# A new order of the sparse-attention stage: turns, conversions and top-k rounds at other places in four queues

## What is computed

```python
h = rms_norm(x, norm_g[l])
proj = h @ w_in[l]
(..., q_b, k_b, v_b, z_b, qi, ki, wi, q_m, z_m, gate) = jnp.split(proj, cuts, axis=-1)
qb = rotary(rms_norm(q_b.reshape(B, S, 8, 128), dsa_q_norm_g[l]), positions)
kb = rotary(rms_norm(k_b.reshape(B, S, 8, 128), dsa_k_norm_g[l]), positions)
y_b = dsa_attention(qb, kb, vb, qib, kib, wib).reshape(B, S, 1024) * jax.nn.silu(z_b)
merged = (g[:, :, 0] * (y_a @ w_branch[l, 0]) + g[:, :, 1] * (y_b @ w_branch[l, 1])
          + g[:, :, 2] * (y_m @ w_branch[l, 2]))
```

## Time and profile before

| | us |
|---|---|
| median of 3 runs | 975.56 |
| lowest, highest | 972.61, 975.66 |
| the profiled execution | 975.56 |
| its span, first to last instruction | 973.5 |
| TensorE busy | 957.0 (98%) |
| VectorE busy | 718.6 (74%) |
| ScalarE busy | 534.5 (55%) |
| GpSimd busy | 351.6 (36%) |
| mean granted TensorE clock | 0.998 |

### The profile page before, as it was taken

The page is one execution under the profiler, slowest core; times in us unless marked ns, Lnnn a source line. Parts: engine busy times, 40 slices in busy tenths (PEclk is TensorE's granted clock), DMA queues, the critical chain, the costliest instruction groups (busy, mean ns, idle before and its releaser), DMA issues.

```text
span 973.5 us, 13407 instructions
## 1 busy us (share of the span) xinstructions
PE 957.0 (98%) x4897; PEld 840.1 (86%) x4897; DVE 718.6 (74%) x1079; ACT 534.5 (55%) x810; POOL 351.6 (36%) x247
## 2 busy tenths in 40 slices
PE   8999999999899999999998999999999999999998
PEld 7888888888778988988987878898998989988887
DVE  6878987686996696696696466796776867735486
ACT  6877645454447547546563321676675857741351
POOL 0200835457055164164130053271623626106600
PEclk9999999999999999999999999999999999999999
DMA  8624222143532432432363234707024150638312
GB/s 282 238 87 130 88 87 87 43 146 115 155 95 65 149 111 66 143 114 70 119 217 130 94 128 157 238 12 215 1 86 142 32 152 1 234 92 310 142 44 86
DMA packets 105156, 119.27 MB, mean 123 GB/s; under 512 B 4772, under 2 KB 80136, under 8 KB 104332
## 3 DMA queue, kind: packets, MB, share of 16 engines
q1 hardware_dynamic: 105084, 118.53, 37.3%
q10 hardware_dynamic: 16, 0.00, 0.0%
HBM read 106.45 MB, written 12.07 MB: 122 GB/s over the span
## 4 chain that ended last, share of the span: by engine, by line
PE 87%; DVE 8%; issue 2%; ACT 1%; DMA 1%; POOL 0%; SPq 0%; DVEq 0%; ACTq 0%
PE proj L780 39%; PE proj L1289 9%; PE proj L1140 9%; PE att L1310 7%; PE proj L1310 5%; PE att L1360 3%; PE proj L950 2%; PE att L1122 2%; PE att L1104 1%; DVE score L2396 1%; PE att L1069 1%; DVE small L2394 1%; PE proj L1246 1%; PE att L1112 1%; PE att L1047 1%
## 5 line engine op out<-in xcount | busy, mean ns | idle before, releaser
L780 PE MATMUL proj<-hT_hi,w_hi 128*128 128x512 f32 x328 | 129.0, 393 | 0.0
L780 PE MATMUL proj<-hT_hi,w_lo 128*128 128x512 f32 x328 | 128.0, 390 | 0.0
L780 PE MATMUL proj<-hT_lo,w_hi 128*128 128x512 f32 x328 | 127.8, 390 | 0.0
L2131 DVE TENSOR_TENSOR w_lo<-w_raw,w_hi 128x2048 fp32r<-128x2048 f32 x28 | 68.6, 2449 | 49.9 <-ACT w_hi L1410 45.8
L1410 ACT ACTIVATE w_hi<-w_raw 128x2048 fp32r<-128x2048 f32 x28 | 53.6, 1914 | 67.7 <-PE proj L780 66.4
L780 PE MATMUL proj<-y_hi,w_hi 128*128 128x512 f32 x192 | 76.2, 397 | 4.9 <-DVE merged L2665 3.3
L780 PE MATMUL proj<-y_lo,w_hi 128*128 128x512 f32 x192 | 75.4, 393 | 0.0
L780 PE MATMUL proj<-y_hi,w_lo 128*128 128x512 f32 x192 | 75.3, 392 | 0.0
L780 PEld LDWEIGHTS proj<-hT_hi,w_lo 128*128 128x128 f32 x328 | 61.5, 188 | 13.0
L780 PEld LDWEIGHTS proj<-hT_lo,w_hi 128*128 128x128 f32 x328 | 61.6, 188 | 12.3
L780 PEld LDWEIGHTS proj<-hT_hi,w_hi 128*128 128x128 f32 x328 | 61.6, 188 | 12.2
(11 more groups left out here) (522 smaller groups left out, 2935.5 us busy)
## 6 DMA issues: line engine op xcount, KB each, us to landing
w_raw<-w_in_in SPq DMA_DIRECT2D x36, 512.0 KB, 4.3
w_raw<-w_in_in SPq DMA_DIRECT2D x56, 256.0 KB, 3.5
w_raw<-w_branch_in SPq DMA_DIRECT2D x10, 1024.0 KB, 5.2
merged<-w_in_in SPq DMA_DIRECT2D x38, 256.0 KB, 3.5
merged<-w_in_in SPq DMA_DIRECT2D x14, 512.0 KB, 5.8
...
```

Of the source, the lines that this page charges most:

```text
L780: ins = mm(ps, lhs[a](k, k0), rhs[b](k, k0), start=(first and k == 0 and j == 0), stop=(last and k == KH - 1 and j == 2))
L2131: V.tensor_tensor(w_lo[:, kh, :, 0:n], w_raw[:, kh, :, 0:n], w_hi[:, kh, :, 0:n].bitcast(F32), ALU.subtract).then_inc(w_lo_done, 1)
```

## The change

No arithmetic is added or taken away; steps are moved in the lists of five engines and waits are set to fit.

- TensorE, panels of pairs 0 to 2: turning q and k of head r moves from slot 3 to 2 and its score from 5 to 4; turning those of head l moves from the start of the next unit to slot 0 of the second panel; turning r's probabilities moves from slot 3 to 1, its values from 5 to 3. Turning l now waits for r's masks (b_masked), the score of l for r's copied probabilities, and turning the probabilities of an even head for the copied q and k of the next one (b_qcopied, b_kcopied).
- TensorE, branch panels 0 and 1: the same kind of exchange for heads 6 and 7.
- ScalarE and VectorE: b_qk_high(l) and b_qk_low(l) move ahead of the probabilities of r; m_exps moves ahead of three bs_split.
- VectorE: b_rotary(r) moves ahead of the low half of operand 8, the low half of operand 10 ahead of b_maxes(r); of the top-k rounds, eight now stand between the low halves of operands 1 and 2 of the first unit and four later in it, and two more stand earlier, in panel BS.
- SP: raw slot c of the first unit is loaded before d; the load of yF before that of merged.
- GpSimd: the token sums for branch A wait for b_y of all eight heads, and no longer for ys_lo.

```diff
--- before.py
+++ after.py
@@ -600,8 +600,8 @@
             sp.wait_ge(w_lo_done, 2 * BS[0] + 2)
             unit_load("b", 0)
             sp.wait_ge(s_low, 3)
+            unit_load("c", 0)
             unit_load("d", 0)
-            unit_load("c", 0)
             sp.wait_ge(m_y, 2 * M_HEADS)
             sp.dma_start(ym_kept[:, 6 * S:8 * S], yF[:, 6 * S:8 * S]).then_inc(kept, 16)
             for b in range(4):
@@ -642,11 +642,11 @@
             load(GB[0], [(wb[2], 0, 512)])
             sp.wait_ge(yb_sent[1], SENT0 + 16 * (PAIRS - 1))
             sp.wait_ge(f_half, HALF0 + 2 * PAIRS - 1)
+            sp.dma_start(yF[:, 0:6 * S], yb_kept).then_inc(late_landed, 16)
             sp.wait_ge(b_rotated, B_HEADS - 1)
             sp.wait_ge(b_vlow, B_HEADS - 1)
             sp.wait_ge(ys_hi, 1)
             sp.dma_start(merged[:, 6 * S:8 * S], ym_kept[:, 6 * S:8 * S]).then_inc(kept_back, 16)
-            sp.dma_start(yF[:, 0:6 * S], yb_kept).then_inc(late_landed, 16)
 
             def sig_loads(q):
                 for b in range(4):
@@ -1087,7 +1087,12 @@
 
             def b_turn_qk(a):
                 pe.wait_ge(b_rotated, a + 1)
-                pe.wait_ge(*((b_pcopied, a * 4) if a else (m_y, 2 * M_HEADS)))
+                if a == 0:
+                    pe.wait_ge(m_y, 2 * M_HEADS)
+                elif a % 2:
+                    pe.wait_ge(b_masked, a * 4)
+                else:
+                    pe.wait_ge(b_pcopied, a * 4)
                 for c in range(2):
                     for t in range(TT):
                         ins = turn(att[c][:, t * P:(t + 1) * P],
@@ -1106,6 +1112,9 @@
                     ins.then_inc(b_scores, 1)
 
             def b_turn_p(a):
+                if a % 2 == 0:
+                    pe.wait_ge(b_qcopied, a + 2)
+                    pe.wait_ge(b_kcopied, a + 2)
                 for t in range(TT):
                     pe.wait_ge(b_scaled, a * 4 + (t + 1))
                     for s in range(t + 1):
@@ -1144,8 +1153,6 @@
             def b_unit(i):
                 main, other = (banks[0], banks[1]), (banks[2], banks[3])
                 tail = 2 * i - 1
-                if i:
-                    b_turn_qk(tail)
                 b_product(i, 0, h_block(0, 0), main, True,
                           lambda t: (bank_empty[t], BF[2][t] + 2 * i) if i else (bank_empty[t], BS[2][t] + 1))
                 if i:
@@ -1197,8 +1204,8 @@
                 b_unit(i)
                 r, l = 2 * i, 2 * i + 1
                 if i < PAIRS - 1:
-                    f_panel(i, 0, (0, P, 2 * P), {3: [lambda: b_turn_qk(r)], 5: [lambda: b_score(r)]})
-                    f_panel(i, 1, (0, P, 2 * P), {3: [lambda: b_turn_p(r)], 5: [lambda: b_values(r)]})
+                    f_panel(i, 0, (0, P, 2 * P), {2: [lambda: b_turn_qk(r)], 4: [lambda: b_score(r)]})
+                    f_panel(i, 1, (0, P, 2 * P), {0: [lambda: b_turn_qk(l)], 1: [lambda: b_turn_p(r)], 3: [lambda: b_values(r)]})
                 else:
                     f_panel(i, 0, (P, 0), {3: [lambda: b_turn_qk(r)]})
 
@@ -1226,9 +1233,9 @@
             pe.wait_ge(bank_empty[0], BF[2][0] + 2 * PAIRS - 1)
             pe.wait_ge(bank_empty[1], BF[2][1] + 2 * PAIRS - 1)
             pe.wait_ge(u_added, 6 * PAIRS)
-            branch_panel(0, y_split(1), {1: [lambda: b_score(r)], 5: [lambda: b_turn_p(r)], 7: [lambda: b_values(r)]})
-            branch_panel(1, None, {0: [lambda: b_turn_qk(l)], 2: [lambda: b_score(l)], 5: [lambda: b_turn_p(l)],
-                                   7: [lambda: b_values(l)]})
+            branch_panel(0, y_split(1), {1: [lambda: b_score(r)], 2: [lambda: b_turn_qk(l)], 4: [lambda: b_turn_p(r)],
+                                         6: [lambda: b_values(r)]})
+            branch_panel(1, None, {0: [lambda: b_score(l)], 3: [lambda: b_turn_p(l)], 5: [lambda: b_values(l)]})
             branch_panel(2, y_split(2))
             branch_panel(3, None)
 
@@ -1765,8 +1772,6 @@
             def b_body(i):
                 n, last = B_OPS * i, i == PAIRS - 1
                 tail, r, l = 2 * i - 1, 2 * i, 2 * i + 1
-                if i:
-                    b_qk_high(tail)
                 b_high(n + 2)
                 if i:
                     act.wait_ge(b_vlow, 2 * i)
@@ -1798,6 +1803,7 @@
                 gate_evac(i, 0)
                 b_exps(r)
                 b_high(n + 11)
+                b_qk_high(l)
                 b_probs_high(r)
                 b_high(n + 12)
                 z_evac(l)
@@ -1805,11 +1811,11 @@
                 gate_evac(i, 1)
 
             split_hi(BS[0], 1, BS[1] + 1, 512, (3, BS[2][3]))
+            m_exps(M_HEADS - 1)
             act.wait_ge(s_made, 1)
             act.wait_ge(m_scores, 2 * M_HEADS)
             for region in (2, 0, 1):
                 bs_split(region)
-            m_exps(M_HEADS - 1)
             m_probs_high(M_HEADS - 1)
             b_high(0)
             act.wait_ge(m_out, 2 * M_HEADS)
@@ -1860,10 +1866,10 @@
             for k in range(4, KT):
                 ym_high(k)
             b_exps(r)
+            b_qk_high(l)
             b_probs_high(r)
             split_hi(GB[0] + 1, 0, GB[1] + 2, 512)
             b_values_high(l)
-            b_qk_high(l)
             split_hi(GB[0] + 1, 1, GB[1] + 2, 512, (3, GB[2][3] + 1))
             b_exps(l)
             b_probs_high(l)
@@ -2558,48 +2564,40 @@
             def b_body(i):
                 n, last = B_OPS * i, i == PAIRS - 1
                 tail, r, l = 2 * i - 1, 2 * i, 2 * i + 1
-
-                def rounds(t, times):
-                    for _ in range(times if i == 0 else 0):
-                        top_round(t)
-
-                if i:
-                    b_qk_low(tail)
                 b_low(n + 2)
-                rounds(1, 4)
                 if i:
                     b_maxes(tail)
                 b_low(n + 3)
                 b_add(i, 1, (banks[2], banks[3]), b_raw[:, 0:2], 1)
                 if i:
                     b_scale_p(tail)
-                rounds(2, 2)
                 b_low(n + 4)
                 if i:
                     b_probs(tail)
-                rounds(2, 2)
                 b_low(n + 5)
                 b_low(n + 6)
                 if i:
                     b_finish(tail)
-                rounds(2, 4)
+                else:
+                    for _ in range(4):
+                        top_round(2)
+                    make_masks()
                 b_add(i, 3, (banks[0], banks[1]), b_fifth, 5)
                 b_low(n + 7)
-                if i == 0:
-                    make_masks()
                 b_add(i, 5, (banks[2], banks[3]), b_second, 3)
+                b_rotary(r)
                 b_low(n + 8)
-                b_rotary(r)
                 b_values_low(r)
                 if last:
                     return
                 b_low(n + 9)
                 b_qk_low(r)
                 b_rotary(l)
+                b_low(n + 10)
                 b_maxes(r)
-                b_low(n + 10)
                 b_scale_p(r)
                 b_low(n + 11)
+                b_qk_low(l)
                 b_probs(r)
                 b_low(n + 12)
                 b_finish(r)
@@ -2607,18 +2605,22 @@
 
             split_lo(BS[0], 1, 512)
             m_norms(M_HEADS - 1)
+            top_round(2)
             for nth, region in enumerate((2, 0, 1)):
                 bs_low_of(region, nth + 1)
             m_scale_p(M_HEADS - 1)
+            top_round(2)
+            m_probs(M_HEADS - 1)
             for _ in range(2):
                 top_round(2)
-            m_probs(M_HEADS - 1)
             b_low(0)
             m_rest(M_HEADS - 1)
             bs_low_of(3, 4)
             b_low(1)
-            for _ in range(2):
+            for _ in range(4):
                 top_round(2)
+            for _ in range(4):
+                top_round(1)
             for i in range(PAIRS):
                 b_body(i)
 
@@ -2678,12 +2680,12 @@
             b_maxes(r)
             for k in range(4, KT):
                 ym_low(k)
+            b_qk_low(l)
             b_scale_p(r)
             b_probs(r)
             split_lo(GB[0] + 1, 0, 512)
             b_finish(r)
             b_values_low(l)
-            b_qk_low(l)
             for b in range(4):
                 branch_merge(0, b)
             split_lo(GB[0] + 1, 1, 512)
@@ -3065,7 +3067,7 @@
                 pool.wait_ge(a_norm_steps, h * 5 + 3)
                 G.tensor_tensor(a_den, a_ss, minus_half[:, 0:TT], ALU.pow).then_inc(a_norm_steps, 1)
 
-            pool.wait_ge(ys_lo, 2 * KT)
+            pool.wait_ge(b_y, B_HEADS)
 
             for f, (k0, t0) in enumerate(((0, HALF_T), (KH, HALF_T), (0, 0), (KH, 0))):
                 hi, lo = h_part(k0, t0)
```

## The result

| | before | after |
|---|---|---|
| median of 4 runs, us | 975.43 | 1018.4 |
| lowest, highest | 972.61, 975.66 | 1015.78, 1019.99 |
| span of the profiled execution | 973.5 | 1014.6 |
| mean granted TensorE clock | 0.998 | 0.983 |

The changed kernel takes 1.0445 times as long (95% interval 1.0413 to 1.0477): 43 us more, against 47.8 forecast.

The account below looks back on a forecast made before the run. TensorE, almost never idle, was taken to bound the kernel by its own instruction stream plus few waits. Terms 4.5 + 9.7 + 18.5 + 2.3 + 8.0 + 4.8 = 47.8 on 975.56 gave 1023.4 us, range 1004 to 1034.

Parts of the forecast that it names:

- Start and first unit: Up to the first unit's end: later exponentials, waits at products 2 and 3, shorter wait for the adds; +4.5 us.
- Pairs 0 to 2: Panels of these pairs: TensorE comes too early for VectorE's rigid chain; +9.7 us in pair 0, +18.5 in pairs 1 and 2.
- the second wait: Second panel of each pair: turning r's probabilities waits 3.7 us for head l's copied q and k.
- the first wait: Slot 0 of each pair's second panel: turning l waits 4.4 us for all four masks of r.
- Last pair and branch panels: Last pair and branch panels: later weights +4.1 us, turn of l +4.0, L2665 waits, clock and gaps -5.8; sum +2.3.
- GpSimd's sums: Branch A sums take turns with VectorE's lows of y at SBUF: TensorE waits 2.8 and 5.2 us; together +8.0.
- The clock: TensorE's granted clock falls behind exposed waits of over 3 us; +4.8 us, or 9.6 if all fall.
- six chances of one half: Falls behind product 3, three waits before r's probabilities, the last turn of l and ys_lo: 0.8 us each.
- the last turn of l: Slot 2 of the branch panels: turning l waits for r's masks, +28.6 against +24.5; +4.0 us.
- (1): Rival: interlocks as forecast but no port loss in the y lows; 1015 us, chance 0.12.
- (2): Rival: looser interlocks, one wait per pair and not two, no clock falls; 996 us, chance 0.10.
- (3): Rival: faster, VectorE's chain short enough, masks ending by +20.2, so the removed waits count; 965 us, chance 0.05.

Follow-up runs that it names:

- experiment one: Kernel before with only the new order of the start and the first unit (exponentials, top-k rounds, masks, slot c before d): 980.95 us, ratio 1.0054.
- Experiment six: Changed kernel with the low half of operand 10 behind the masks of r again in pairs 0 to 2: 1015.66 us, ratio 1.0413.
- experiment five: Changed kernel with GpSimd's wait for the sums of branch A put back to ys_lo: 1009.8 us, ratio 1.0366.
- Experiments eight: Changed kernel with 11 (pair 0) and 16 (pairs 1 and 2) unused matmuls ahead of TensorE's wait for the masks: 1019.45 us, ratio 1.0455.
- nine: Kernel before with 9 unused matmuls behind the turn of l in branch panel 1: 973.74 us, ratio 0.9994.
- experiment four: Kernel before with only GpSimd's wait for the sums of branch A changed from ys_lo to b_y of all heads: 986.59 us, ratio 1.0129.
- experiments two: Kernel before with only the new places of the steps in the panels of pairs 0 to 2: 1000.72 us, ratio 1.0272.
- three: Kernel before with only the new order of the last pair and of branch panels 0 and 1: 977.14 us, ratio 1.0024.
- ten: Kernel before with only the rotation of r ahead of the low half of operand 8, in pairs 0 to 2: 974.32 us in one run.

## Why the prediction was right

The four parts measured alone add up to 5.8 + 25.6 + 2.0 + 11.5 = 44.9, the whole to 43.0. Point by point:

- **Start and first unit**, forecast +4.5, alone +5.8. The order of the waits was right (1.9, 3.5 and 1.7 forecast; 2.2, 3.0 and 1.9 measured there, 0.9 for the last head of M against 1.4). What is missing is one clock fall, which the term did not have: behind product 3 in experiment one (0.67 over 3.5 us), behind product 2 in the changed kernel.
- **Pairs 0 to 2**, forecast 9.7 + 18.5 = 28.2, alone 25.6. The chain was read nearly to the point: masks at +24.6 forecast and +24.3 measured, copies of l at +31.9 and +31.5. It is why the pair term held although its split did not: the second wait is 0.7 to 2.1 us, not 3.7, because TensorE, slowed behind the first wait, used up part of it. Experiment six shows a term that I had not seen as one: 1.75 us of the low half of operand 10 stood in an idle stretch before, and ahead of the masks it is on the chain (+29.4 without it, +31.5 with it, to the turn of the probabilities); I had put it into the sum without noting that it could be had back.
- **Last pair and branch panels**, forecast +2.3, alone +2.0. Inside, the weights came as forecast: ScalarE split them from 535.9, 5.1 behind the request, and VectorE's low half of them ended at 540.2, +17.0 from the start of the pair's panel (523.15) where +17.1 was forecast. But the branch panels also need a bank that ScalarE empties, and its copies stand behind that split in its list; they end at 541.2, and the branch panels start at +18.2 (541.30 - 523.15). Behind that wait the clock fell (0.65 over 4.2 us). So TensorE came to the turn of l at +27.4 in place of +24.5, and the turn waited 0.9 us in place of 4.0. The masks themselves came where forecast, +28.3 against +28.6.

```profile
530.87 0.93 SPq L491 DMA_DIRECT2D w_raw<-w_branch_in  x2
...
535.92 1.92 ACT L1417 ACTIVATE w_hi<-w_raw 128x2048 fp32r<-128x2048 f32 x1 [10.00 <-issue]
...
541.30 0.47 PE L780 MATMUL proj<-y_hi,w_hi 128*128 128x512 f32 x1 [2.13 <-ACT arena L1756]
```

  The releaser named is ScalarE's copy of a bank; ScalarE had stood 10 us at the split ahead of it in its list, for the load. The of before have the same step with 1.17 us.
- **GpSimd's sums**, forecast +8.0 with waits of 2.8 and 5.2; measured 7.7 by experiment five, as waits of 2.2 and 2.6, a clock fall and small change. The price of one low beside GpSimd, 2.88 against 0.68 alone, is about what the forecast took from the lows of 1024 columns (2.4 more for each turn). The Trainium skill (SBUF — State Buffer, "SBUF: two separate sides") calls the shared ports an exclusive lock held for a whole instruction; the trace agrees, since 2.88 is about a low of 0.6 and then a GpSimd instruction of 2.3.
- **The clock**, forecast +4.8 from six chances of one half. This is the mis-sized term: the mean granted clock says 15.3. None of the six places that I named had a fall in the trace (the clock is 1.00 behind product 3, the three turns of probabilities, the last turn of l and y_lo); eight others had: product 2, the turn of r in pair 0, three turns of l, the wait for operand 8 and the first and third branch panel. The three turns of l are the plainest miss: I had forecast 4.4 us of wait at each, longer than all but one on my list, and left them out of the count without a reason. Nor is the list of places fixed: product 3 had a fall in the traces of experiments one, six and eight, a turn of the probabilities in those of five, six and eight. That the total still came out within 5 us of the medians is luck in part: the waits that I had too long (11.1 us for the probabilities against 4.6 measured, 4.0 against 0.9 at the last turn of l, 5.2 against 2.6 at y_lo) stand against the falls that I had too few. Both have in part one origin. A fall between two waits on the same late engine is paid out of the second wait, so the two may not be added: the sum had to be made from arrival times, or with falls only where no wait follows. Experiments eight (0 won) and nine (1.6 won in the trace) show the two cases apart, eight in pair 1, where no second fall disturbs the comparison.

The Trainium skill (TensorE: Matmul & The Clock Gate, "What's actually happening") ties the low clock to idle time; all falls here lie behind waits, but not behind every wait. By its rule alone as I used it the clock term would have been 9.6, nearer, and still added where it is not paid.

Of the rivals, (1), no loss at the port, is refuted by experiments four and five, (2) by the two waits per pair. (3) would have needed masks by +20.2; they came at +24.3.

What stays open: why product 3 and pair 0 differ by 1 to 3 us between executions of kernels whose lists are the same there (product 3 waited 1.4 in the changed kernel and 3.0 in experiment one). In the two traces a clock fall ahead of it explains it; what decides whether that fall comes, none of the runs shows. The same holds in the kernel before: behind the adds' wait of 2.8 us, in lists that are the same up to there, the clock fell in the traces of experiments two, three, nine and ten and stayed at 1.00 in those of before and of experiment four.
